# Attention scores on the two halves of TensorE's rows: near beside far products, and two sparse units together

## Chip, cores and metric

The kernel runs on one core of a Trainium2 chip. The metric is the device time of one execution in microseconds (us). TensorE multiplies, VectorE (DVE) and ScalarE (ACT) work on its results, SyncE (SP) issues the loads of weights; GpSimd (POOL) does nothing.

## What is computed

The program is three blocks on an activation of 512 positions by 1024 features in f32: a convolution layer, a layer of dilated attention, and a layer with a sparse attention and an mLSTM between two feed-forward parts. The change touches two spots.

The dilated attention has 8 heads of 64 features in each of three groups (window, dilation): (128, 1), (512, 4), (2048, 16). A softmax for each group, weighted over the groups by their log denominators, is the same as one softmax over all keys of the three groups:

```python
s = jnp.einsum('bdnqhc,bdnkhc->bdnhqk', qb, kk) * (hd ** -0.5)
s = jnp.where(valid[:, None], s, NEG_INF)      # 0 <= dist <= band, in the residue's own subsequence
...
wts = jax.nn.softmax(jnp.stack(lses, axis=0), axis=0)
o = jnp.sum(wts[..., None] * jnp.stack(outs, axis=0), axis=0)
```

The sparse attention has 8 query heads on 2 heads of keys; every query attends its 128 best keys by an index score:

```python
score = jnp.einsum('bqhs,bqh->bqs', jax.nn.relu(jnp.einsum('bqhd,bsd->bqhs', iq_blk, ik)), iw_blk)
top_s, top_i = lax.top_k(score, k_sel)
s = jnp.einsum('bqgrd,bqkgd->bqgrk', q_blk, kg) * att_scale
```

## The kernel before

Each engine has one instruction stream, written out by hand; counters (semaphores) order them, and an engine waits in place, with all that is queued behind. Weight tiles of 128 x 1024 come through a ring of four: SyncE loads a tile, ScalarE copies its high part (`prep`, L444), VectorE subtracts to get the low part (L953), and TensorE makes 24 matmuls of 512 columns of it (`tile`, L1570).

**Dilated attention (stage 4).** Heads are taken two at a time, in four chunks; the two heads of a chunk lie on partitions 0 to 63 and 64 to 127 of `at_raw`. A chunk has 10 slots `j`, each with one weight tile of the input projection for chunk `c`, while the attention of the chunk before, `a = c - 1`, goes on beside it; the fourth attention chunk (`c == 4`) has no tiles beside it. An attention chunk has 8 units: unit `u` is head `u // 4` and residue `r = u % 4`, the 128 queries `r, r + 4, ...`. A unit's scores (`unit_scores`, L1753) are one near product, 128 queries by all 512 keys of group 0 into one PSUM bank (L1770), and two far products of 128 by 128 for groups 1 and 2 into the next bank (L1772). Both contract over 64 features, so they use half of TensorE's 128 rows, the head's own half; operands with a step of four are read as they lie.

VectorE adds the mask, scales, and takes the maximum of all 768 scores in one `tensor_tensor_reduce` (L1245), and negates it (L1248, `m_done`). ScalarE exponentiates with the row sum (L688, `e_done`); VectorE takes the reciprocal and scales (L1268, L1269, `p_done`). TensorE transposes the six blocks (L1798, `t_done`), ScalarE copies them to `at_PT`, and TensorE multiplies with the values (L1789). In slot `j` TensorE does, after the tile, the values of unit `j - 2`, the transposes of unit `j - 1`, the scores of unit `j`, and then a transpose of values (L1842) or a sum of squares (`sum_squares`, L1621). The scores of a unit wait for `m_done` of the unit before, whose bank they take; in the fourth chunk there are two homes, and the wait is for the unit before that.

In the slots behind a tile of queries or keys VectorE also makes the head norm and the rotary turn: L975 on the sum of squares, L968 to L970 (Newton, after ScalarE's guess L473, L474), L1276 to L1279 (`n_done`); tiles of values and gates it evacuates at L1265 and L1260. ScalarE copies a raw tile, squares it, and issues four DMAs that swap rows into `at_pair` (L725); from the third tile on the issue waits for `n_done` of the tile two before. Tiles of queries and keys are 0, 1, 3, 4, 5, 6 of a chunk; of values 2, 7, 8; of gates 9.

**Sparse attention (stage 10).** 32 units, `SPARSE_UNITS`, by block `b` of 128 queries (keys 0 to 128 (b + 1)), head column `c` and half: successive units lie on alternating halves. Iteration `u` of TensorE has the transposes of `u` (L2040), `scores(u + 2)` (L1950, product at L1955, after `m_done` of unit `u`), a weight tile if `u` is in `FILL`, and the values of `u - 1` (L2056). VectorE has in iteration `u` `normalise(u + 1)` (L1370), `masked(u + 2)` (L1357), the tile's low part and rounds of the top selection. The first two units' scores stand together in stage 9. The index scores (L1945) alternate halves too.

Of the kernel before, what the change touches and what calls it, by code (L numbers as in the profile page):

```python
# [19 lines left out]
P = 128  # L20
S = 512
# [10 lines left out]
HEAD = 64  # L32
# [110 lines left out]
TIMES = {"chunk": 4 * len(QK_TILES), "unit": 4 * UNITS}  # L143


def build(nc, weights, x_in, ple_in, pos_in, params_in, consts_in, masks_in, out, spill):
    ctx = ExitStack()
    with ctx:
# [41 lines left out]
        with ExitStack() as s_first:  # L190
# [3 lines left out]
            with ExitStack() as s_conv:  # L194
# [8 lines left out]
            (at_raw, at_pair, at_mask, at_T, at_SG, at_Sm, at_PT, at_st, at_Yh, at_Yl, at_V) = scope(  # L203
                ("at_raw", [P, 12, S], F32), ("at_pair", [P, 2, S], F32), ("at_mask", [P, 4, 768], F32),
                ("at_T", [P, 2, S], F32), ("at_SG", [P, 2, S], F32),
                ("at_Sm", [P, 768], F32), ("at_PT", [P, 768], F32), ("at_st", [P, 4, 4], F32),
# [59 lines left out]
        s_done = sem("s_done")  # L266
        m_done = sem("m_done")
# [52 lines left out]
        def unit_home(a, u):  # L320

            if a == 3 and u % 2:
                return 0, at_raw[:, 0:2, :].rearrange("p a s -> p (a s)")[:, 0:768]
            return 2, at_Sm[:, :]
# [43 lines left out]
        def attention_over(k, chunk=(), unit=()):  # L368

            for kind, sems in (("chunk", chunk), ("unit", unit)):  # L370
                for s in sems:
                    k.n[s] = k.n.get(s, 0) + TIMES[kind]

# [51 lines left out]
        def _(act):  # L425
# [242 lines left out]
            act.dma_start(at_mask[:, :, :], masks_in).then_inc(mask_loaded, 16)  # L668
            k.up(dve_out)
            normed = k.n[n_done]  # L670
            for c in range(5):
                a = c - 1
                for j in range(SLOTS):
# [5 lines left out]
                    for step in ((1, 2) if c == 4 else (2, 1)):  # L679
# [5 lines left out]
                        else:  # L685
                            act.wait_ge(m_done, UNITS * a + j)
                            st, probs = at_st[:, (j - 1) % 4, :], unit_home(a, j - 1)[1]
# [251 lines left out]
        def _(dve):  # L939
# [293 lines left out]
            for c in range(5):  # L1233
                a = c - 1
                for j in range(SLOTS):
                    if c < 4 and j - 1 in SUM_SLOT:
                        head_var(1)
                    if a >= 0 and 0 <= j - 1 < UNITS:
                        u = j - 1
                        st = at_st[:, u % 4, :]  # L1240
                        if u == 0 and a == 0:
                            dve.wait_ge(mask_loaded, 16)
                        dve.wait_ge(s_done, UNITS * a + u + 1)
                        bank, probs = unit_home(a, u)
                        link(dve.tensor_tensor_reduce(  # L1245
                            out=probs, in0=flat(ps[:, bank:bank + 2, :])[:, 0:768], in1=at_mask[:, u % 4, :],
                            scale=HEAD ** -0.5, scalar=TAKEN, op0=ALU.add, op1=ALU.max, accum_out=st[:, 0:1]))
                        dve.tensor_scalar(st[:, 1:2], st[:, 0:1], -1.0, None, ALU.mult).then_inc(m_done, 1)  # L1248
# [17 lines left out]
                    if a >= 0 and 0 <= j - 1 < UNITS:  # L1266
                        dve.wait_ge(e_done, UNITS * a + u + 1)
                        link(dve.reciprocal(st[:, 3:4], st[:, 2:3]))  # L1268
                        dve.tensor_scalar(probs, probs, st[:, 3:4], None, ALU.mult).then_inc(p_done, 1)  # L1269
# [14 lines left out]
            attention_over(k, unit=(s_done, m_done, e_done, p_done, t_done, o_done))  # L1284
# [267 lines left out]
        def _(pe):  # L1552
# [200 lines left out]
            def unit_scores(a, j):  # L1753

                if a < 0 or j >= UNITS:
                    return
                rows, r = slice(HEAD * (j // 4), HEAD * (j // 4) + HEAD), j % 4
                if j == 0:
                    pe.wait_ge(n_done, normed + len(QK_TILES) * (a + 1))
                elif a < 3:  # L1760
                    pe.wait_ge(m_done, UNITS * a + j)
                elif j == 1:
                    pe.wait_ge(read_out, k.at(read_out))
                    pe.wait_ge(v_copied, GROUPS * 4)
                    pe.wait_ge(var_done, 4 * len(QK_TILES))
                else:
                    pe.wait_ge(m_done, UNITS * a + j - 1)
                bank = unit_home(a, j)[0]
                q = 6 * (a % 2)
                pe.matmul(ps[:, bank, :], at_raw[rows, q, r:S:4], at_raw[rows, q + 1, :], start=True, stop=True)  # L1770
                for g in (1, 2):
                    mm = pe.matmul(ps[:, bank + 1, (g - 1) * P:g * P], at_raw[rows, q + 2 * g, r:S:4],  # L1772
                                   at_raw[rows, q + 2 * g + 1, r:S:4], start=True, stop=True)
                mm.then_inc(s_done, 1)

            def unit_values(a, j):

                if 0 <= j - 2 < UNITS:
                    u = j - 2
                    rows, r = slice(HEAD * (u // 4), HEAD * (u // 4) + HEAD), u % 4  # L1780
# [13 lines left out]
                if 0 <= j - 1 < UNITS:  # L1794
                    pe.wait_ge(p_done, UNITS * a + j)
                    probs = unit_home(a, j - 1)[1]
# [15 lines left out]
            for c in range(5):  # L1812
                a = c - 1
                for j in range(SLOTS):
# [12 lines left out]
                    if c == 4:  # L1827
                        unit_scores(a, j)
                    if a >= 0:
                        unit_values(a, j)  # L1830
                    if 0 <= a < 3:
                        unit_scores(a, j)
# [18 lines left out]
            attention_over(k, unit=(s_done, m_done, p_done, t_done, pt_done, o_done), chunk=(r0_done, rs_done, n_done, var_done))  # L1851
# [98 lines left out]
            def scores(u):  # L1950
                c, half, b = SPARSE_UNITS[u]
                rows = slice(HEAD * half, HEAD * half + HEAD)
                if u >= 2:
                    pe.wait_ge(m_done, k.up(m_done))
                pe.matmul(ps[:, 4 + u % 2, 0:P * (b + 1)], ds_U[rows, c, b * P:(b + 1) * P],  # L1955
# [79 lines left out]
            for u in range(33):  # L2035
# [8 lines left out]
                if u < 30:  # L2044
                    scores(u + 2)
# [212 lines left out]
```

## Time and profile before

| | us |
|---|---|
| median of three runs | 2011.47 (2009.0 to 2016.49) |
| profiled execution | 2012.62 |
| its span | 2010.8 |
| TensorE matmuls busy | 1948.5 (97%) |
| weight loads | 1515.0 (75%) |
| VectorE | 1245.3 (62%) |
| ScalarE | 862.2 (43%) |
| mean granted clock of TensorE | 0.985 |

The profile gives for each instruction its start and length. PE is TensorE's matmul side, PEld its weight loads; an f32 product is two passes, each a load and a matmul record. Matmul records overlap with their successors by 0.07 us or more, so what a group costs is read from its start to the start of what follows. A granted clock of 1.00 is 2.4 GHz, of 0.50 1.2 GHz. The idle time before an instruction stands in brackets with what ended it.

### The profile page before, as it was taken

The numbers are of one execution on the slowest core, as the hardware profiler recorded it, in microseconds if no ns is written. First come the engines' busy times: TensorE is split into PE (matmuls) and PEld (weight loads), VectorE is DVE, ScalarE is ACT, GpSimd is POOL, SyncE is SP. The second block draws the span as 40 slices with busy tenths as digits, with TensorE's granted clock in tenths as the row PEclk, the third lists the DMA queues.
The fourth block names the chain that finished last, engine by engine and source line by source line (L and its number), as shares of the span: only waits on it lengthen the run. The fifth ranks groups of instructions, "written<-read, shape, count | busy, mean of one in ns | idle before, by whom it ended". The sixth has DMA issues, their size and how long they took to land.

```text
span 2010.8 us, 23124 instructions
## 1 busy us (share of the span) xinstructions
PE 1948.5 (97%) x8436; PEld 1515.0 (75%) x8436; DVE 1245.3 (62%) x1864; ACT 862.2 (43%) x1175; POOL 0.2 (0%) x4
## 2 busy tenths in 40 slices
PE   6999899899999999999999999999999999999999
PEld 4888687677777777888888876666766788888887
DVE  5999888757575738644443365588666555444322
ACT  5444555444444435544432234455343444434221
POOL 0000000000000000000000000000000000000000
PEclk9999999999999989999999999999999999999999
DMA  4333243221212112323333332112221223233333
GB/s 176 101 95 95 74 131 121 85 69 50 65 56 66 48 53 95 97 91 104 94 94 121 120 95 74 53 42 63 74 64 42 95 93 106 94 103 95 101 99 105
DMA packets 49281, 175.70 MB, mean 87 GB/s; under 512 B 6064, under 2 KB 6192, under 8 KB 48432
## 3 DMA queue, kind: packets, MB, share of 16 engines
q1 hardware_dynamic: 44640, 160.19, 25.5%
q10 hardware_dynamic: 4560, 14.41, 2.1%
q8 instruction: 53, 0.87, 0.2%
q14 instruction: 28, 0.23, 0.0%
HBM read 166.71 MB, written 6.29 MB: 86 GB/s over the span
## 4 chain that ended last, share of the span: by engine, by line
PE 72%; DVE 20%; ACT 5%; issue 2%; DMA 1%; ACTq 1%; DVEq 0%
PE ps L1570 58%; DVE cv_acc L1132 6%; DVE w_lo L953 3%; PE ps L1770 2%; PE ps L1621 2%; PE ps L1798 1%; PE ps L1772 1%; PE ps L1586 1%; PE ps L1789 1%; PE ps L1955 1%; ACT w_hi L435 1%; PE ps L2056 1%; DMA X<-x 1%; PE ps L1945 1%; DVE X L1005 1%
## 5 line engine op out<-in xcount | busy, mean ns | idle before, releaser
L953 DVE TENSOR_TENSOR w_lo<-w_raw,w_hi 128x1024 fp32r<-128x1024 f32 x299 | 365.6, 1224 | 365.1 <-ACT w_hi L435 359.2
L1570 PE MATMUL ps<-H_hi,w_hi 128*128 128x512 f32 x1272 | 509.4, 401 | 1.1 <-DVE H_lo L999 1.1
L1570 PE MATMUL ps<-H_hi,w_lo 128*128 128x512 f32 x1272 | 496.1, 390 | 0.0
L1570 PE MATMUL ps<-H_lo,w_hi 128*128 128x512 f32 x1272 | 496.0, 390 | 0.0
L435 ACT ACTIVATE w_hi<-w_raw 128x1024 fp32r<-128x1024 f32 x299 | 313.5, 1050 | 244.1 <-PE ps L1570 168.8
L1570 PEld LDWEIGHTS ps<-H_hi,w_hi 128*128 128x128 f32 x1272 | 239.5, 188 | 57.9 <-issue 7.4
L1570 PEld LDWEIGHTS ps<-H_lo,w_hi 128*128 128x128 f32 x1272 | 239.4, 188 | 55.3 <-issue 6.7
L1570 PEld LDWEIGHTS ps<-H_hi,w_lo 128*128 128x128 f32 x1272 | 239.2, 188 | 51.0
L1570 PE MATMUL ps<-mid_hi,w_lo 128*128 128x512 f32 x352 | 138.7, 394 | 0.0
L1570 PE MATMUL ps<-mid_hi,w_hi 128*128 128x512 f32 x352 | 138.7, 394 | 0.0
L1570 PE MATMUL ps<-mid_lo,w_hi 128*128 128x512 f32 x352 | 138.7, 394 | 0.0
L1570 PE MATMUL ps<-N_hi,w_hi 128*128 128x512 f32 x280 | 118.4, 423 | 0.7 <-ACT ds_P L815 0.7
L1132 DVE SCALAR_TENSOR_TENSOR cv_acc<-cv_a,par,cv_acc 128x509 f32<-128x509 f32 (+21 forms) x176 | 115.8, 725 | 1.6 <-ACT cv_acc L586 1.6
L1570 PE MATMUL ps<-N_lo,w_hi 128*128 128x512 f32 x280 | 111.6, 399 | 0.0
L1570 PE MATMUL ps<-N_hi,w_lo 128*128 128x512 f32 x280 | 111.5, 398 | 0.0
L435 ACT ACTIVATE mid_hi<-tmp 128x512 f32 x44 | 27.8, 632 | 193.2 <-DVE tmp L1090 193.2
L1570 PEld LDWEIGHTS ps<-mid_hi,w_hi 128*128 128x128 f32 x352 | 65.8, 187 | 16.5
L1570 PEld LDWEIGHTS ps<-mid_hi,w_lo 128*128 128x128 f32 x352 | 65.8, 187 | 16.2
L1570 PEld LDWEIGHTS ps<-mid_lo,w_hi 128*128 128x128 f32 x352 | 65.8, 187 | 16.2
L1086 DVE TENSOR_TENSOR tmp<-ps,rx 128x512 f32<-128x512 f32 x44 | 30.4, 691 | 66.1 <-PE ps L1570 66.1
L1570 PEld LDWEIGHTS ps<-N_hi,w_hi 128*128 128x128 f32 x280 | 53.4, 191 | 23.3 <-issue 9.5
L1570 PEld LDWEIGHTS ps<-N_lo,w_hi 128*128 128x128 f32 x280 | 53.4, 191 | 13.8 <-issue 2.4
(337 smaller groups left out, 2705.3 us busy)
## 6 DMA issues: line engine op xcount, KB each, us to landing
w_raw<-weights SPq DMA_DIRECT2D x299, 512.0 KB, 3.5
X<-x ACTq DMA_DIRECT2D x4, 512.0 KB, 11.3
pl_P<-spill ACTq DMA_DIRECT2D x1, 2048.0 KB, 7.9
spill<-X ACTq DMA_DIRECT2D x8, 256.0 KB, 2.0
X<-spill ACTq DMA_DIRECT2D x2, 1024.0 KB, 5.0
out<-X SPq DMA_DIRECT2D x8, 256.0 KB, 4.6
at_mask<-masks ACTq DMA_DIRECT2D x1, 1536.0 KB, 6.0
at_pair<-at_raw ACTq DMA_DIRECT2D x96, 16.0 KB
```

The costliest lines, as they stand in the source:

```text
L435: return act.activation(out_ap, in_ap, ACT.Copy)
L953: dve.tensor_tensor(w_lo[:, s, :], w_raw[:, s, :], w_hi[:, s, :].bitcast(F32), ALU.subtract)\
L1005: dve.scalar_tensor_tensor(X[:, m:m + n, :], src, scale, X[:, m:m + n, :], ALU.mult, ALU.add)\
L1086: dve.tensor_tensor(tmp[:, j, :], ps[:, bank_of(k.n["prep"] - AHEAD - 1), :], rx[:, :], ALU.mult).then_inc(read_out, 1)
L1132: instr = dve.scalar_tensor_tensor(acc, a[:, 0:S - t], w, acc, ALU.mult, ALU.add)
L1570: mm = pe.matmul(ps[:, bank, :], w, x, start=first and n == 0 and q == 0, stop=last and n == len(blocks) - 1 and q == 2)
L1586: mm = pe.matmul(ps[:, banks[which], :], w, x[:, b, :], start=b == 0 and q == 0, stop=b == KC - 1 and q == 2, skip_group_check=True)
L1621: pe.matmul(ps[:, bank, :], ones if lhsT is None else lhsT, sq[:, (k.n[sq_done] - 1) % 2, :], start=c == 0, stop=c == n - 1).then_inc(sq_u ...
L1770: pe.matmul(ps[:, bank, :], at_raw[rows, q, r:S:4], at_raw[rows, q + 1, :], start=True, stop=True)
L1772: mm = pe.matmul(ps[:, bank + 1, (g - 1) * P:g * P], at_raw[rows, q + 2 * g, r:S:4], at_raw[rows, q + 2 * g + 1, r:S:4], start=True, stop= ...
L1789: mm = pe.matmul(ps[rows, 6, r * P + q0:r * P + q1], at_V[:, 3 * (a % 2) + g, v * P + rows.start:v * P + rows.stop], at_PT[:, b * P + q0:b ...
L1798: mm = pe.transpose(ps[:, 4 + b // 4, (b % 4) * P:(b % 4 + 1) * P], probs[:, b * P:(b + 1) * P], ident)
```

## The change

In the dilated attention a unit `u` is now head `u % 2` and residue `u // 2` (`unit_rows`). TensorE's stream has nine steps -1 to 7 in a chunk: step `v` has the near product of unit `v + 1` and the far products of unit `v`, which lie on different halves of the rows and in different banks. Step -1 stands at the end of slot 9 of the chunk before. A near product waits for `near_done` of the bank's last reader, the far ones for `m_done`. VectorE reduces the near and the far part in two instructions, in successive slots, and joins the two maxima. The probabilities have two buffers in the first three chunks, three in the fourth. The mask is held as `at_near` (4 x 512) and one `at_far` (256) and comes in two DMAs. In the sparse attention `two_scores` makes the products of two units one behind the other, at even `u`, after `m_done` of both units before.

```diff
-TIMES = {"chunk": 4 * len(QK_TILES), "unit": 4 * UNITS}
+TIMES = {"chunk": 4 * len(QK_TILES), "unit": 4 * UNITS, "step": 4 * (UNITS + 1)}
...
-            (at_raw, at_pair, at_mask, at_T, at_SG, at_Sm, at_PT, at_st, at_Yh, at_Yl, at_V) = scope(
-                ("at_raw", [P, 12, S], F32), ("at_pair", [P, 2, S], F32), ("at_mask", [P, 4, 768], F32),
+            (at_raw, at_pair, at_near, at_far, at_T, at_SG, at_Sm, at_PT, at_st, at_Yh, at_Yl, at_V) = scope(
+                ("at_raw", [P, 12, S], F32), ("at_pair", [P, 2, S], F32), ("at_near", [P, 4, S], F32), ("at_far", [P, 2 * P], F32),
                 ("at_T", [P, 2, S], F32), ("at_SG", [P, 2, S], F32),
-                ("at_Sm", [P, 768], F32), ("at_PT", [P, 768], F32), ("at_st", [P, 4, 4], F32),
+                ("at_Sm", [P, 2, 768], F32), ("at_PT", [P, 768], F32), ("at_st", [P, 4, 4], F32),
...
         def unit_home(a, u):
 
-            if a == 3 and u % 2:
-                return 0, at_raw[:, 0:2, :].rearrange("p a s -> p (a s)")[:, 0:768]
-            return 2, at_Sm[:, :]
+            if a == 3 and u % 3 == 2:
+                return at_raw[:, 0:2, :].rearrange("p a s -> p (a s)")[:, 0:768]
+            return at_Sm[:, (u % 3 if a == 3 else u % 2), :]
+
+        def unit_rows(u):
+            return slice(HEAD * (u % 2), HEAD * (u % 2) + HEAD), u // 2
+
+        def near_bank(a, u):
+            return 0 if a == 3 and u >= 3 and u % 2 else 2
+
+        def far_bank(a, u):
+            return 1 if a == 3 and u % 2 else 3
...
-            act.dma_start(at_mask[:, :, :], masks_in).then_inc(mask_loaded, 16)
+            act.dma_start(at_near[:, :, :], masks_in[:, :, 0:S]).then_inc(mask_loaded, 16)
+            act.dma_start(at_far[:, :], masks_in[:, 0, S:S + 2 * P]).then_inc(mask_loaded, 16)
...
-                    if a >= 0 and 0 <= j - 1 < UNITS:
+                    if a >= 0 and 0 <= j <= UNITS:
                         u = j - 1
-                        st = at_st[:, u % 4, :]
-                        if u == 0 and a == 0:
-                            dve.wait_ge(mask_loaded, 16)
-                        dve.wait_ge(s_done, UNITS * a + u + 1)
-                        bank, probs = unit_home(a, u)
-                        link(dve.tensor_tensor_reduce(
-                            out=probs, in0=flat(ps[:, bank:bank + 2, :])[:, 0:768], in1=at_mask[:, u % 4, :],
-                            scale=HEAD ** -0.5, scalar=TAKEN, op0=ALU.add, op1=ALU.max, accum_out=st[:, 0:1]))
-                        dve.tensor_scalar(st[:, 1:2], st[:, 0:1], -1.0, None, ALU.mult).then_inc(m_done, 1)
+                        if u < 0 and a == 0:
+                            dve.wait_ge(mask_loaded, 32)
+                        dve.wait_ge(s_done, (UNITS + 1) * a + j + 1)
+                        if u >= 0:
+                            st, probs = at_st[:, u % 4, :], unit_home(a, u)
+                            link(dve.tensor_tensor_reduce(
+                                out=probs[:, S:S + 2 * P], in0=ps[:, far_bank(a, u), 0:2 * P], in1=at_far[:, :],
+                                scale=HEAD ** -0.5, scalar=TAKEN, op0=ALU.add, op1=ALU.max, accum_out=st[:, 3:4]))
+                            dve.wait_ge(near_done, UNITS * a + u + 1)
+                            link(dve.tensor_tensor(st[:, 0:1], st[:, 0:1], st[:, 3:4], ALU.max))
+                            dve.tensor_scalar(st[:, 1:2], st[:, 0:1], -1.0, None, ALU.mult).then_inc(m_done, 1)
+                        if j < UNITS:
+                            dve.tensor_tensor_reduce(
+                                out=unit_home(a, j)[:, 0:S], in0=ps[:, near_bank(a, j), :], in1=at_near[:, j // 2, :],
+                                scale=HEAD ** -0.5, scalar=TAKEN, op0=ALU.add, op1=ALU.max,
+                                accum_out=at_st[:, j % 4, 0:1]).then_inc(near_done, 1)
...
-            def unit_scores(a, j):
-
-                if a < 0 or j >= UNITS:
-                    return
-                rows, r = slice(HEAD * (j // 4), HEAD * (j // 4) + HEAD), j % 4
-                if j == 0:
-                    pe.wait_ge(n_done, normed + len(QK_TILES) * (a + 1))
-                elif a < 3:
-                    pe.wait_ge(m_done, UNITS * a + j)
-                elif j == 1:
-                    pe.wait_ge(read_out, k.at(read_out))
-                    pe.wait_ge(v_copied, GROUPS * 4)
-                    pe.wait_ge(var_done, 4 * len(QK_TILES))
-                else:
-                    pe.wait_ge(m_done, UNITS * a + j - 1)
-                bank = unit_home(a, j)[0]
+            def step_scores(a, v):
+
+                near, far = (v + 1 if v + 1 < UNITS else None), (v if v >= 0 else None)
                 q = 6 * (a % 2)
-                pe.matmul(ps[:, bank, :], at_raw[rows, q, r:S:4], at_raw[rows, q + 1, :], start=True, stop=True)
-                for g in (1, 2):
-                    mm = pe.matmul(ps[:, bank + 1, (g - 1) * P:g * P], at_raw[rows, q + 2 * g, r:S:4],
-                                   at_raw[rows, q + 2 * g + 1, r:S:4], start=True, stop=True)
+                if near is not None:
+                    rows, r = unit_rows(near)
+                    if near == 0:
+                        pe.wait_ge(n_done, normed + len(QK_TILES) * a + 2)
+                    if a == 3 and near == 3:
+                        pe.wait_ge(read_out, k.at(read_out))
+                    elif UNITS * a + near:
+                        pe.wait_ge(near_done, UNITS * a + near - (a == 3 and near > 3))
+                    mm = pe.matmul(ps[:, near_bank(a, near), :], at_raw[rows, q, r:S:4], at_raw[rows, q + 1, :],
+                                   start=True, stop=True)
+                if far is not None:
+                    rows, r = unit_rows(far)
+                    if far == 0:
+                        pe.wait_ge(n_done, normed + len(QK_TILES) * (a + 1))
+                    if a == 3 and far == 1:
+                        pe.wait_ge(v_copied, GROUPS * 4)
+                        pe.wait_ge(var_done, 4 * len(QK_TILES))
+                    elif UNITS * a + far:
+                        pe.wait_ge(m_done, UNITS * a + far - (a == 3 and far > 1))
+                    for g in (1, 2):
+                        mm = pe.matmul(ps[:, far_bank(a, far), (g - 1) * P:g * P], at_raw[rows, q + 2 * g, r:S:4],
+                                       at_raw[rows, q + 2 * g + 1, r:S:4], start=True, stop=True)
                 mm.then_inc(s_done, 1)
...
-                    rows, r = slice(HEAD * (u // 4), HEAD * (u // 4) + HEAD), u % 4
+                    rows, r = unit_rows(u)
...
-                    if c == 4:
-                        unit_scores(a, j)
+                    if c == 4 and j < UNITS:
+                        step_scores(a, j)
                     if a >= 0:
                         unit_values(a, j)
-                    if 0 <= a < 3:
-                        unit_scores(a, j)
+                    if 0 <= a < 3 and j < UNITS:
+                        step_scores(a, j)
...
+                    if c < 4 and j == SLOTS - 1:
+                        step_scores(c, -1)
...
-            def scores(u):
-                c, half, b = SPARSE_UNITS[u]
-                rows = slice(HEAD * half, HEAD * half + HEAD)
-                if u >= 2:
-                    pe.wait_ge(m_done, k.up(m_done))
-                pe.matmul(ps[:, 4 + u % 2, 0:P * (b + 1)], ds_U[rows, c, b * P:(b + 1) * P],
-                          ds_kvi[rows, 0, 0:P * (b + 1)], start=True, stop=True).then_inc(s_done, 1)
-                k.up(s_done)
+            def two_scores(first):
+
+                if first:
+                    pe.wait_ge(m_done, k.up(m_done, 2))
+                for u in (first, first + 1):
+                    c, half, b = SPARSE_UNITS[u]
+                    rows = slice(HEAD * half, HEAD * half + HEAD)
+                    pe.matmul(ps[:, 4 + u % 2, 0:P * (b + 1)], ds_U[rows, c, b * P:(b + 1) * P],
+                              ds_kvi[rows, 0, 0:P * (b + 1)], start=True, stop=True).then_inc(s_done, 1)
+                    k.up(s_done)
...
-                if u < 30:
-                    scores(u + 2)
+                if u < 30 and u % 2 == 0:
+                    two_scores(u + 2)
```

The counters' totals in `attention_over` and the callers of `unit_home` follow.

## Rows read from the trace of the kernel before

**Rows 1.** Stretches: length, then busy us (records) by engine, granted clock, DMA share, GB/s.

```profile
412.70:508.70 96.00, 94.53 (x458) 73.90 (x457) 63.15 (x104) 43.89 (x65) 0.00 (x0) 1.00 0.21 62
...
700.40:720.90 20.50, 19.88 (x78) 14.93 (x78) 7.91 (x21) 6.43 (x11) 0.00 (x0) 0.50 0.00 1
...
1484.90:1576.40 91.50, 86.77 (x415) 58.27 (x414) 53.27 (x143) 42.26 (x86) 0.00 (x0) 1.00 0.14 42
```

**Rows 2.** The chain of waits between 540 and 600 us: start, length, what.

```profile
551.78 5.47 PE ps L1570 x24
...
572.67 5.49 PE ps L1570 x24
...
578.98 0.63 DVE at_Sm L1269
```

**Rows 3.** Timeline of one unit's scores, TensorE and its weight loads: start, length.

```profile
528.12 1.24 PE L1770 MATMUL ps<-at_raw 64*128 64x512 f32 x2
...
529.21 1.08 PE L1772 MATMUL ps<-at_raw 64*128 64x128 f32 x4
...
530.22 1.13 PE L1621 MATMUL ps<-sq,con 128*128 128x512 f32 x2
...
528.78 1.21 PEld L1772 LDWEIGHTS ps<-at_raw 64*128 64x128 f32 x4
```

**Rows 4.** Timeline, TensorE: sparse and index scores, with transposes and values.

```profile
1251.89 0.49 PE L1945 MATMUL ps<-ds_kvi,X 64*128 64x256 f32 x2
...
1415.16 0.49 PE L1955 MATMUL ps<-ds_kvi,X 64*128 64x128 f32 x4
...
1427.79 0.48 PE L1955 MATMUL ps<-ds_kvi,X 64*128 64x128 f32 x2
...
1550.08 0.66 PE L2040 MATMUL ps<-con,ds_P 128*128 128x128 f32 x4
...
1550.66 1.12 PE L1955 MATMUL ps<-ds_kvi,X 64*128 64x512 f32 x2
...
1551.72 1.09 PE L2056 MATMUL ps<-ds_PT,ds_kvi 128*64 128x128 f32 x8
```

**Rows 5.** Groups by line and shape, VectorE: busy us, mean ns, idle before.

```profile
L1245 DVE CUSTOM_DVE_ANT_0 at_Sm<-ps,at_mask 128x768 f32<-128x768 f32 x28 | 26.8, 957 | 13.4 <-PE ps L1772 12.7
...
L1248 DVE TENSOR_SCALAR at_st<-at_st 128x1 f32<-128x1 f32 x32 | 4.9, 154 | 1.1
...
L1364 DVE CUSTOM_DVE_ANT_0 ds_P<-ps,ds_acc 128x512 f32<-128x512 f32 x8 | 5.5, 686 | 7.3 <-PE ps L1955 7.3
...
L1364 DVE CUSTOM_DVE_ANT_0 ds_P<-ps,ds_acc 128x256 f32<-128x256 f32 x8 | 3.4, 420 | 3.9 <-PE ps L1955 3.9
```

**Rows 6.** Timeline of slots 5 to 7, VectorE and ScalarE (ACTq issues DMAs).

```profile
555.98 0.69 DVE L968 TENSOR_TENSOR rs<-r 128x512 f32<-128x512 f32 x1 [0.37 <-ACT r L474]
...
560.93 2.62 ACTq L725 DMA_DIRECT2D at_pair<-at_raw  x4
...
572.50 2.62 ACTq L725 DMA_DIRECT2D at_pair<-at_raw  x4
...
577.71 0.19 ACT L688 ACTIVATION_READ_ACCUMULATOR at_Sm<-at_Sm,at_st 128x1 f32 x1
```

**Rows 7.** Timeline of the fourth chunk's units, TensorE.

```profile
701.02 1.54 PE L1798 MATMUL ps<-con,at_Sm 128*128 128x128 f32 x6 [2.00 <-DVE at_Sm L1269]
...
702.49 2.09 PE L1770 MATMUL ps<-at_raw 64*128 64x512 f32 x2
...
721.08 1.25 PE L1770 MATMUL ps<-at_raw 64*128 64x512 f32 x2
...
725.00 1.25 PE L1770 MATMUL ps<-at_raw 64*128 64x512 f32 x2
```

**Rows 8.** Timeline, VectorE: reductions of two successive sparse units.

```profile
1558.88 0.68 DVE L1364 CUSTOM_DVE_ANT_0 ds_P<-ps,ds_acc 128x512 f32<-128x512 f32 x1
...
1561.23 0.68 DVE L1364 CUSTOM_DVE_ANT_0 ds_P<-ps,ds_acc 128x512 f32<-128x512 f32 x1
```

More of the change, by code:

```diff
@@ L266, in build @@
         s_done = sem("s_done")
+        near_done = sem("near_done")
         m_done = sem("m_done")
@@ L366, in build, with attention_over @@
         V0 = GROUPS * 4
-        def attention_over(k, chunk=(), unit=()):
-            for kind, sems in (("chunk", chunk), ("unit", unit)):
+        def attention_over(k, chunk=(), unit=(), step=()):
+            for kind, sems in (("chunk", chunk), ("unit", unit), ("step", step)):
                 for s in sems:
@@ L686, in _ @@
                             act.wait_ge(m_done, UNITS * a + j)
-                            st, probs = at_st[:, (j - 1) % 4, :], unit_home(a, j - 1)[1]
+                            st, probs = at_st[:, (j - 1) % 4, :], unit_home(a, j - 1)
                             act.activation(probs, probs, ACT.Exp, bias=st[:, 1:2], accum_out=st[:, 2:3])\
@@ L1266, in _ @@
                     if a >= 0 and 0 <= j - 1 < UNITS:
+                        st, probs = at_st[:, u % 4, :], unit_home(a, u)
                         dve.wait_ge(e_done, UNITS * a + u + 1)
@@ L1283, in _ @@
             gate(3)
-            attention_over(k, unit=(s_done, m_done, e_done, p_done, t_done, o_done))
+            attention_over(k, unit=(near_done, m_done, e_done, p_done, t_done, o_done), step=(s_done,))
             stage_end(dve, "dve", k, 4)
@@ L1795, in unit_values @@
                     pe.wait_ge(p_done, UNITS * a + j)
-                    probs = unit_home(a, j - 1)[1]
+                    probs = unit_home(a, j - 1)
                     for b in range(6):
@@ L1850, in _ @@
                         sum_squares(0, 1, 1, head_ones)
-            attention_over(k, unit=(s_done, m_done, p_done, t_done, pt_done, o_done), chunk=(r0_done, rs_done, n_done, var_done))
+                    if c < 4 and j == SLOTS - 1:
+                        step_scores(c, -1)
+            attention_over(k, unit=(near_done, m_done, p_done, t_done, pt_done, o_done), step=(s_done,), chunk=(r0_done, rs_done, n_done, var_done))
             k.up(split_lo, 4)
@@ L1962, in _ @@
                     pe.wait_ge(n_done, k.at(n_done, 5))
-                    scores(0)
-                    scores(1)
+                    two_scores(0)
                 if s_ < len(MIX_TILES):
```

## Prediction

> **What bounds the kernel now.** I first cut the execution into stretches, to see which engine is full where the change acts. In a chunk of the dilated attention TensorE is busy for 94.5 of 96.0 us, VectorE for 63; in the second part of the sparse attention TensorE for 86.8 of 91.5 [rows 1]. TensorE's instruction stream is the bound, so time taken out of it counts until another engine's chain becomes the last to arrive. The chain of waits shows where that is near: it runs through TensorE, tile after tile (551.78, 572.67), and leaves it in this piece only for VectorE's evacuation and scaling of the probabilities, ahead of the transposes (0.63 at 578.98) [rows 2]. Then I read what a score group costs, and whether two row halves ever ran together.
>
> **The score products of the dilated attention.** A unit's near product begins at 528.12, its two far ones at 529.21, the next work at 530.22 [rows 3]: near 1.09, far 1.01, together 2.10 us, and 8 x 2.10 = 16.8 a chunk. Each product is two passes, a weight load before each; the far products' four loads span 1.21 us [rows 3], more than their columns need.
>
> Do two halves run at once? The kernel already contains such pairs. The first two sparse units (halves 0 and 1, nothing waited for between) take 0.49 us for four passes of 128 columns; one unit's two passes take 0.48 [rows 4]. In the index scores two passes of 256 columns began together and both took 0.49 [rows 4]. So pairs of equal size are free in their second member. The change's main pair is unequal, 512 columns beside two times 128, with strided weights: no row shows that. Its bounds are 1.09 (the near product alone) and 2.10 (nothing overlaps). I take 1.2: the far side's four loads become the longer stream, 1.21, and the equal pairs speak for the low end. A near or a far step alone I also put at 1.2, since neither now has the other to hide its first load and its tail.
>
> A chunk then has one near step alone (moved to slot 9 of the chunk before), seven pairs and one far step alone: 9 x 1.2 = 10.8, gross 6.0 saved.
>
> **What VectorE pays.** One reduction over 768 columns costs 0.957 us; two over 512 and 256 cost 0.686 + 0.420 (rows of the same operation in the sparse part), with a second accumulator read (0.08) and one more one-column operation (0.15, by the negation's row) [rows 5]: 1.34 + gaps instead of 0.96, +0.4 us a unit. It is hidden mostly: the negated maximum comes after the 256 columns, so ScalarE's exponential starts no later, and the near reduction runs while VectorE would wait for ScalarE (0.37 idle before L968) [rows 6]. If that cover were gone it would be 32 x 0.4 = 13 us. The new wait on near_done holds a product that needs its bank read; that reduction is done in the same VectorE slot, 5.5 us of weight tile earlier, in the first three chunks. The wait of VectorE on its own near_done is for work of the slot before: nothing.
>
> **What is late next.** In slots 5 and 6 ScalarE issues its four row-swap DMAs only when VectorE's rotary chain of an earlier tile has ended: issue at 560.93 and again at 572.50 [rows 6], 11.57 us apart, while the TensorE slot is 10.45 (two slots from 551.78 to 572.67) [rows 2]. This loop has no score product in it. It ends in the exponential, read out at 577.90; evacuation, reciprocal and scaling follow, and the probabilities could be ready near 579.0 instead of 579.6. TensorE alone would come 2 x 0.9 earlier. So of 1.8 us about 0.7 stays; 1.1 is given back as longer waits around slot 7. A chunk nets 6.0 - 1.1 = 4.9; three chunks **14.7 us**.
>
> The fourth chunk has no weight tiles beside it. Its start gains nothing: step -1, near reduction (0.7), then the first pair are in series, and the first transposes wait 2.00 us already (701.02) [rows 7]. Behind them stand six units' scores. At full clock a cycle of one unit is 3.92 us (721.08 to 725.00) [rows 7]; without 0.9 it would be 3.0, which is also VectorE's and ScalarE's chain (far reduction to maximum 0.9, exponential 1.1, scaling 0.9), so 0.9 is all there is. TensorE is at 1.2 GHz there for 20.5 us (granted 0.50) [rows 1], where a near product takes 2.09 instead of 1.25 [rows 7]; the shorter cycle puts more units into that stretch. 6 x 0.9 = 5.4, less 1.4 for that: **4.0 us**.
>
> **The sparse attention.** A single unit's score takes 1.06 us at 512 columns (1550.66 to 1551.72) and 0.42 at 128 [rows 4], between them by width 0.63 and 0.84. The first pair is a pair already. Of the other 15 pairs one member each goes: 3 x 0.42 + 4 x 0.63 + 4 x 0.84 + 4 x 1.06 = 11.4 gross. In the first eight units a weight tile stands in each, and their four pairs (1.9) are kept whole. For units 10 to 15 VectorE's rounds of the top selection end last: I count nothing. Beyond, VectorE's loop takes 2.35 us a unit (1558.88 to 1561.23) [rows 8], TensorE's 2.65 (score 1.06; values 1.09 and transposes 0.66, each less 0.07 of overlap with its successor) [rows 4]; a pair would bring it to 2.12, so only 0.30 of each 0.53 counts, 57% of 7.6 = 4.3. The new wait at even units, for the second unit's maximum, ends about 0.1 to 0.3 us behind the transposes where VectorE is late (reduction 0.69, negation 0.15) and costs nothing elsewhere; some 0.2 in all. 1.9 + 4.3 - 0.2: **6.0 us**, between 2 and 11.4.
>
> **Edits at nothing.** The mask in two DMAs (1.5 MB becomes 1.15, needed a chunk later); the third probability buffer; the new order of the units over halves and residues, which changes no size.
>
> **Sum.** 14.7 + 4.0 + 6.0 = 24.7 us from the profiled execution's 2012.6, which is 1.1 above the median of the runs: 1987.9, or 1987 against that median. A change under 0.5% (10 us) could not be told from none.
>
> **Rivals.** (1) *Passes keep their order of issue*: then a far pass can't begin before near's second, and the pair costs 1.09 / 2 + 1.01 = 1.55. A pair saves 0.55, a chunk 7 x 0.55 - 0.3 = 3.6, the four 14 less 3 for the start of the last and slots 5 to 7; the sparse pairs half, 3. Together 14: 1998. Against it: two index passes started within 0.01 us, while one unit's two passes are 0.21 apart (0.48 for two of 0.27), so those two were different heads, out of order [rows 4]. Chance 0.08. The Trainium skill states this rule in TensorE: Matmul & The Clock Gate, "The mechanism": starts and ends of matmuls follow program order and only weight loads are pulled ahead. By it the sum would be this rival's; the trace disagrees with it.
>
> (2) *The unequal, strided pair doesn't overlap*; the sparse ones do. Then the dilated part pays its rearrangement: the last chunk's serial start and the lost hiding, about +3, against -6: 2009. For it: no such pair in the trace. Chance 0.06.
>
> (3) *Slower, through the clock.* In the last chunk TensorE idled 2.00 us and its clock was at 1.2 GHz for the next 20.5 [rows 1, 7]. The same may follow the longer wait at slot 7 of three chunks, where today's short wait grows to some 1.5, split by the values. It decides once the idle time there comes to about 2 us. At 1.2 GHz a stretch of tiles does half its work: 10 us lost each, 31 for three, against 24.7: 2018. Against it: the chunks before are at full clock [rows 1] with such waits in them. Chance 0.04. If each lasts only a third as long, 10 us go: 1997, chance 0.06.
>
> **Numbers.** Forecast 0.76, its own range 1980 to 1995. Range of all: 1979 (near and far at the lower bound, more of the sparse 11.4) to 2001, which takes in rival 1 and the short clock falls and leaves out 2 and the long ones. Faster by over 0.5%: 0.76 + 0.07 + 0.05 = 0.88; within: rival 2 and edges 0.08; slower: 0.04.
>
> **What would show it.** Right: L1770's successor and the far matmuls starting together, pair to next work 1.1 to 1.3; chunk pitch 91 instead of 95.9; waits before the transposes or values at slot 7 grown to 1 to 2 us in all; the last chunk's unit cycle 3.0 to 3.2 at full clock; sparse units in pairs of one unit's duration. Wrong: far passes starting after near's second (rival 1) or after its end (2); granted clock under 0.95 in a chunk (3); or VectorE's reductions ending later than ScalarE's exponential, which would make the +0.4 a unit visible.

## The result, and the profile after

The changed kernel takes 1987.82 us (median of 4 runs, 1986.31 to 1989.35) against 2011.49 (2009.0 to 2016.49) for the kernel before: ratio 0.9873, 95% interval 0.9848 to 0.9898, 23.7 us less. The forecast was 1987.0, in a range of 1979 to 2001. The total came out right; two of its terms did not, and they nearly cancel. The profiled executions were 1.1 us above the median before and 1.5 below it after, so the traces differ by 26.3 us and not by 23.7.

The head of the page of the kernel after, to be held against the kernel before (span 2010.8, TensorE 1948.5 us, VectorE 1245.3):

```profile
span 1984.5 us, 23259 instructions
...
PE 1916.2 (97%) x8436; PEld 1495.0 (75%) x8436; DVE 1252.0 (63%) x1960; ACT 861.3 (43%) x1175; POOL 0.2 (0%) x4
```

TensorE has as many matmuls as before and is busy for 32 us less, for the most part because two of them now share a stretch of time; VectorE has 96 instructions and 7 us more. The changed pair itself, timeline of TensorE in the second attention chunk (start, length, with the line, shape and count), read in windows so narrow that passes are not merged. Line 1784 is the near product (1770 before), 1796 the far ones (1772), 1822 the transposes, 1640 the sum of squares, which comes next:

```profile
525.47 0.82 PE L1784 MATMUL ps<-at_raw 64*128 64x512 f32 x1
525.47 0.59 PE L1796 MATMUL ps<-at_raw 64*128 64x128 f32 x1
525.89 0.41 PE L1796 MATMUL ps<-at_raw 64*128 64x128 f32 x1
526.12 0.59 PE L1784 MATMUL ps<-at_raw 64*128 64x512 f32 x1
526.12 0.41 PE L1796 MATMUL ps<-at_raw 64*128 64x128 f32 x1
526.36 0.41 PE L1796 MATMUL ps<-at_raw 64*128 64x128 f32 x1
526.70 1.13 PE L1640 MATMUL ps<-sq,con 128*128 128x512 f32 x2
```

From 525.47 to 526.70 the pair takes 1.23 us; before, a unit's products took 2.10 [rows 3]. The near product's first pass and a far pass begin together at 525.47; a second far pass begins at 525.89, ahead of the near product's second at 526.12; the other two far ones begin at 526.12 and 526.36. The program issues both near passes before any far one, so the starts of passes on different row halves do not follow the program's order.

Stretches of the kernel after, with the columns of [rows 1]. The first goes from the tile of slot 0 in the second attention chunk to the same tile a chunk later; the others are the pieces at half clock between 405 and 740 us:

```profile
502.04:593.19 91.15, 89.04 (x458) 69.62 (x457) 64.97 (x128) 43.43 (x66) 0.00 (x0) 1.00 0.21 63
...
482.90:486.30 3.40, 3.40 (x7) 1.99 (x7) 3.26 (x6) 0.00 (x0) 0.00 (x0) 0.50 0.01 2
667.20:670.60 3.40, 3.40 (x9) 2.33 (x8) 3.26 (x6) 0.00 (x0) 0.00 (x0) 0.50 0.02 5
687.70:697.90 10.20, 8.05 (x34) 5.27 (x32) 6.33 (x24) 4.19 (x7) 0.00 (x0) 0.50 0.00 0
```

Between the same two tiles, with the same 458 matmuls, the kernel before takes 95.96 us (502.99 to 598.95): the chunk gains 4.8 us. But there are two short pieces at 1.2 GHz, at 482.9 and 667.2, in chunks that were wholly at 2.4 GHz before, and the long one in the fourth chunk is 10.2 us instead of 20.5.

What TensorE waits for between 360 and 760 us (waited for: us in total, times, longest), first in the kernel before, then after:

```profile
PE ps L1798 <- DVE at_Sm L1269: 6.4, 10, 2.0
PE ps L1842 <- DVE var L975: 4.3, 2, 4.1
PE ps L1621 <- DVE var L975: 2.1, 1, 2.1
PE ps L1789 <- ACT at_PT L435: 1.2, 1, 1.2
PE ps L1808 <- DVE at_Yl L1012: 0.3, 1, 0.3
```

```profile
PE ps L1822 <- DVE at_Sm L1288: 5.4, 9, 0.8
PE ps L1866 <- DVE var L986: 4.6, 2, 4.1
PE ps L1784 <- DVE at_st L1263: 2.9, 2, 2.2
PE ps L1640 <- DVE var L986: 2.1, 1, 2.1
PE ps L1605 <- DVE G_lo L1010: 2.1, 1, 2.1
PE ps L1813 <- ACT at_PT L445: 1.9, 4, 0.9
```

New are the wait of the near product on VectorE's near reduction (the serial start of the fourth chunk) and, in each of the first three chunks, a wait of the values on ScalarE. (The wait on `G_lo` is not new: the kernel before has it at 764.48, outside this window.) Slot 7 in the first attention chunk, timeline of TensorE:

```profile
478.72 1.09 PE L1813 MATMUL ps<-at_PT,at_V 128*64 128x128 f32 x12 [0.37 <-ACT at_PT L445]
480.62 0.88 PE L1822 MATMUL ps<-con,at_Sm 128*128 128x128 f32 x6 [0.80 <-DVE at_Sm L1288]
481.42 1.30 PE L1796 MATMUL ps<-at_raw 64*128 64x128 f32 x4
482.64 1.90 PE L1640 MATMUL ps<-sq,con 128*128 128x512 f32 x2
```

The waits are 0.37 + 0.80 = 1.17 us, and the work behind the far products, from 482.64, is at half speed (two passes in 1.90 us; 1.12 in the second chunk). ScalarE's issue loop, rows of its timeline after:

```profile
555.45 2.62 ACTq L736 DMA_DIRECT2D at_pair<-at_raw  x4
...
567.01 2.62 ACTq L736 DMA_DIRECT2D at_pair<-at_raw  x4
```

11.56 us apart, as in [rows 6] (11.57), while two TensorE slots there now take 9.59 each: the loop has not moved.

The fourth chunk at full clock, timeline of TensorE, first pass of three successive near products; the cycle is 3.06 us, against 3.92 in [rows 7]:

```profile
698.75 0.81 PE L1784 MATMUL ps<-at_raw 64*128 64x512 f32 x1
...
701.81 0.82 PE L1784 MATMUL ps<-at_raw 64*128 64x512 f32 x1
...
704.86 0.82 PE L1784 MATMUL ps<-at_raw 64*128 64x512 f32 x1
```

And a pair of sparse units with 512 columns each, four passes where [rows 4] had two in 1.12; the next work begins 1.06 us after them:

```profile
1528.34 1.13 PE L1983 MATMUL ps<-ds_kvi,X 64*128 64x512 f32 x4
1529.40 1.09 PE L2083 MATMUL ps<-ds_PT,ds_kvi 128*64 128x128 f32 x8
1531.57 0.66 PE L2067 MATMUL ps<-con,ds_P 128*128 128x128 f32 x4 [1.08 <-DVE ds_P L1393]
```

**Where the time went.** I read the start of the same weight tile in both traces, profiled execution against profiled execution (26.3 us less span). From the tile at 398.98 before (399.69 after) to the one at 687.72 (677.47) the three chunks gain 0.71 + 10.25 = 11.0 us. The fourth chunk, from there to 743.11 (724.04), gains 8.8. The sparse units gain 6.6. The three sum to 26.4. Behind waits of 1.14 and 1.54 us on VectorE's scaling, the sparse stretch of this trace has a short piece at half clock of its own:

```profile
1483.00:1486.40 3.40, 3.40 (x9) 2.63 (x9) 1.65 (x5) 1.92 (x4) 0.00 (x0) 0.50 0.00 0
```

The profiles of experiments 3, 4 and 5 have the same sparse code and the same two waits, and no such piece there; between the same tiles they gain 7.6, 8.05 and 7.96 us.

### The profile page after: what moved, and what is told of

The parts are those of the page before. It is cut to its first block, busy times and chain, and to the rows that moved or that the text cites. A ratio compares the mean times of both kernels' runs of the same rounds, so it can differ in the third digit from the quotient of the medians.

```text
span 1984.5 us, 23259 instructions
## 1 busy us (share of the span) xinstructions
PE 1916.2 (97%) x8436; PEld 1495.0 (75%) x8436; DVE 1252.0 (63%) x1960; ACT 861.3 (43%) x1175; POOL 0.2 (0%) x4
## 4 chain that ended last, share of the span: by engine, by line
PE 75%; DVE 16%; ACT 5%; issue 2%; ACTq 2%; DMA 1%; DVEq 0%
PE ps L1589 63%; DVE w_lo L964 2%; PE ps L1605 2%; ACTq L736 1%; PE ps L1640 1%; ACT w_hi L445 1%; PE ps L1784 1%; PE ps L1822 1%; PE ps L1813 1%; PE ps L1796 1%; DVE cv_acc L1143 1%; DMA X<-x 1%; DVE rs L980 1%; DVE rs L981 1%; PE ps L1971 1%
```

## The experiments

Each is timed against the kernel before on the same chip. "Dilated gain" and "sparse gain" are read at the same tiles as above.

**1. Dilated part alone.** The sparse attention has its single scores back.

```
-                if u < 30 and u % 2 == 0:
-                    two_scores(u + 2)
+                if u < 30:
+                    scores(u + 2)
```

> The dilated part as changed, the sparse scores one unit at a time as before. If the two parts are independent, the time is 6.6 us over the changed kernel's (the sparse stretch's loss in the two traces): 1994, and the 64 sparse passes run two by two again, 1.12 for 512 columns. If the gain of the two parts were shared (one clock state, one chain), it would be under 3 or over 10.

Measured: 1994.07 us, ratio 0.9903 (0.9876 to 0.993). Dilated gain 19.9, sparse gain 0.

**2. Sparse part alone.** The kernel before, with `two_scores` for its `scores` and the wait for two maxima.

> The sparse part as changed, the dilated one as before. Independent parts: 2011.5 - 6.6 = 2005. With the whole gross of 11.4 (if VectorE took nothing back) 2000. The stretch from the first score to the last transposes should be that of the changed kernel to 0.5 us.

Measured: 2005.31 us, ratio 0.9961 (0.9946 to 0.9977). Sparse gain 6.6. By the ratios the two parts save 1.0% and 0.4%, the change 1.3%: they do not touch each other.

**3. The new schedule without the overlap.** All steps, waits and split reductions of the change stay, but near and far units lie mostly on the same row half (one of the seven pairs of a chunk has both halves).

```
-            return slice(HEAD * (u % 2), HEAD * (u % 2) + HEAD), u // 2
+            return slice(HEAD * (u // 4), HEAD * (u // 4) + HEAD), u % 4
```

(and the mask of near scores is indexed by `j % 4`).

> The changed kernel with the units in the old order of halves (head u // 4, residue u % 4), so that near and far of a step lie on the same half, but for one step in eight; everything else of the change stays: the steps, the waits, the split reductions, the moved near step. If the overlap of halves makes the gain, a step costs 2.1 again, the chunk 95.5 to 97 instead of 91.2, and the time is 2005 to 2008 (the sparse 6.6 stays), some 3 us over the rival's bound of the old dilated part. If the rearrangement makes it, the time stays near 1988. If passes keep their order of issue, a step of different halves would cost 1.55 in the changed kernel, and this one would be only 9 us slower than it.

Measured: 2003.63 us, ratio 0.995 (0.9932 to 0.9968), 16 us slower than the change. The same instructions in the same order now run one after the other:

```profile
529.15 1.24 PE L1784 MATMUL ps<-at_raw 64*128 64x512 f32 x2
530.23 1.08 PE L1796 MATMUL ps<-at_raw 64*128 64x128 f32 x4
531.24 0.70 PE L1640 MATMUL ps<-sq,con 128*128 128x512 f32 x1
```

From 529.15 to 531.24 is 2.09 us, the price of before. So the gain comes from the two halves. The dilated gain is 5.0 us. In each of the first three chunks the rearrangement loses 1.33 us in slot 9, where a near product now stands alone, and gets 0.87 back in slot 7, where the far ones do; the one pair on both halves adds 0.87. So without any pair a chunk would lose 0.46 us; with the one it gains 0.41, 1.2 over three. The other 3.8 us come in the fourth chunk, whose piece at half clock was 13.7 us instead of 20.5 (experiment 6 shows what such a difference is worth). The rest of this run's gain is the sparse part's 7.6.

**4. A third row-swap buffer.** If ScalarE's issue loop gives back what slots 5 to 7 save, a third buffer should loosen it.

```
-                            if n >= 2:
-                                act.wait_ge(n_done, normed + n - 1)
+                            if n >= 3:
+                                act.wait_ge(n_done, normed + n - 2)
```

(the buffers become `n % 3`, with their semaphores).

> The changed kernel with a third buffer for the row swap, so that ScalarE's four DMAs wait for the rotary chain of three tiles before, not two. If that loop is what gives back 1.1 us a chunk, the waits of TensorE at slot 7 (0.33 before the values, 0.80 before the transposes) fall to the 0.49 of the tile's evacuation, a chunk becomes 0.7 to 0.9 shorter, 2.4 us over three, and the two idle times of TensorE in the first projection chunk (2.1 and 4.1 us, slots 7 and 8), if they hang on the same loop, go too: 1979 to 1983. If VectorE's added 0.4 us a unit is what comes late, nothing changes: 1988.

Measured: 1973.31 us, ratio 0.98 (0.9783 to 0.9818), 14.5 us below the change and 6 below the expectation. The two profiled executions differ by 11.7 us: 14.0 are gained between 379 us and the start of the fourth chunk, and 2.3 are lost elsewhere, where the code is the same and the clock fell at other places. TensorE's waits between 360 and 760 us:

```profile
PE ps L1827 <- DVE at_Sm L1293: 4.4, 9, 0.5
PE ps L1789 <- DVE at_st L1268: 3.1, 2, 2.3
PE ps L1610 <- DVE G_lo L1014: 2.1, 1, 2.1
PE ps L1871 <- DVE var L990: 1.1, 2, 0.8
PE ps L1818 <- ACT at_PT L449: 0.9, 1, 0.9
```

The wait on ScalarE's probabilities is left only in the fourth chunk, none of those behind VectorE's scaling is longer than 0.5, and one stretch of the page shows what that did to the clock (columns as in [rows 1]):

```profile
400.00:675.00 275.00, 269.78 (x1381) 210.83 (x1379) 196.05 (x388) 134.41 (x198) 0.00 (x0) 1.00 0.21 64
```

No piece at half clock is left in the three chunks. As the expectation put it with an "if", the waits of 2.1 and 4.1 us on the variance, in slots 7 and 8 of the projection chunk ahead of them in both kernels, are the same loop: 0.3 us of them is left. What was not expected is the clock: with the half clock behind these waits gone too, they brought 8.5 us, and the three chunks gave another 5.4: two short falls at 1.7 and three times 0.33 + 0.31 of waits.

**5. More work for VectorE.** One more operation over 256 columns behind each near reduction.

```
+                            dve.tensor_tensor(at_spare[:, 0:2 * P], at_far[:, :], at_far[:, :], ALU.add)
```

> The changed kernel with one more VectorE operation a unit (256 columns into a spare place, about 0.4 us), right behind the near reduction: the change's own added cost once more, 32 x 0.4 = 13 us of VectorE. If VectorE's added work is hidden but at slot 7, a chunk grows by 0.3 to 0.5 in its waits there, 1 to 2 us in all: 1989 to 1990. If VectorE is the bound, it grows by up to 13: 2000. If it is hidden everywhere: 1988.

Measured: 1988.6 us, ratio 0.9887 (0.987 to 0.9903), within the spread of the change's own runs. TensorE's wait on ScalarE's probabilities goes from 1.9 to 2.9 us over four places, the serial start of the fourth chunk from 2.9 to 3.5, the rest is as before. So of 13 us more work for VectorE 1.6 us show as waits and the rest is hidden. The total does not show them, also because this profile has a short fall of the clock in the first attention chunk only, one fewer than the change's, and none in the sparse part.

**6. The third buffer in the kernel before.** Is the loop a bound that the change uncovered, or an old one?

> The kernel before the change with the third buffer for the row swap. The changed kernel gained 14.5 us by it: 9 in the first projection chunk (idle time and a low clock behind it) and 5.5 in the other chunks and their clock. If the loop through ScalarE's DMAs became late only by the change's shorter slots, the other chunks gain nothing here and only the first does: 2011.5 - 9 = 2002 to 2003. If the loop held the old kernel as well, the gain is the same 14.5: 1997.

Measured: 2000.2 us, ratio 0.9937 (0.9921 to 0.9954). It gains 8.5 us between 379 and 407 us, in slots 7 and 8 of the projection chunk ahead of the attention; then nothing to 688 us; then 4.5 in the fourth chunk. So beside the attention the loop was just in time before, and only the shorter slots of the change make it late. The stretches at those slots, kernel before and then this one:

```profile
387.00:397.00 10.00, 6.59 (x26) 4.81 (x26) 6.64 (x10) 3.16 (x4) 0.00 (x0) 0.98 0.21 59
396.60:403.40 6.80, 5.17 (x15) 4.23 (x16) 6.56 (x11) 3.97 (x5) 0.00 (x0) 0.50 0.24 77
```

```profile
387.00:397.00 10.00, 9.69 (x45) 7.75 (x44) 9.66 (x15) 4.68 (x6) 0.00 (x0) 1.00 0.34 101
396.60:403.40 6.80, 6.80 (x33) 5.67 (x32) 4.65 (x7) 2.25 (x4) 0.00 (x0) 1.00 0.26 75
```

45 matmuls instead of 26 in the first ten microseconds, and a full clock behind them. The 4.5 us in the fourth chunk have no edit to explain them: its code is that of before. Its piece at half clock was 10.2 us instead of 20.5.

```profile
690.80:701.00 10.20, 8.21 (x33) 6.01 (x32) 5.06 (x15) 3.78 (x7) 0.00 (x0) 0.50 0.00 0
```

**7 and 8. The late selection rounds left out,** in the changed kernel and in the one before. Both leave out VectorE's top-selection rounds that stand at units 8, 10, 12 and 14, so that their selection is incomplete; it costs that much less.

```
-                **{u: ((3, 2),) for u in (8, 10, 12, 14)}, 17: ((3, 1),), 20: ((3, 1),)}
+                17: ((3, 1),), 20: ((3, 1),)}
```

> The changed kernel without the eight top selection rounds of units 8, 10, 12 and 14 (for the last block of queries). If they are what kept the pairs of units 10 to 15 from gaining, the stretch from unit 8's tile to the end of the sparse scores gets shorter by more than in the kernel before (next run): sparse gain 8.0 to 8.5 instead of 6.6; this kernel 3 to 4 us under the changed one.

> The kernel before without the same eight rounds. TensorE waited for VectorE there 0.47 and 1.08 us: it gets 1.5 us shorter, 2010. If the rounds have nothing to do with the pairs' loss, it gains as much as the changed kernel does by it.

Measured: 1982.87 us, ratio 0.9853 (0.9833 to 0.9873), and 2011.21, 0.9991 (0.998 to 1.0002). Between the same sparse tiles the first gains 11.9 us on the unaltered kernel before, more than the 8.0 to 8.5 expected, the second 2.0: without the rounds the pairing brings 9.9 us instead of 6.6. Not all of the difference is the rounds': the profile of number 7 has no half clock in this stretch, that of the change has the piece at 1483. Against the 8.0 of experiments 4 and 5, which have none either, the rounds hold back 1.9 us. Waits of TensorE on the scaled probabilities between 1390 and 1580 us, kernel after and then with the rounds left out:

```profile
PE ps L2067 <- DVE ds_P L1393: 6.0, 7, 1.5
```

```profile
PE ps L2067 <- DVE ds_P L1393: 2.9, 4, 1.1
```

These two runs were worth as much for the clock, since their dilated part is untouched code. Number 8 repeats the kernel before in it. It has a short fall in the second attention chunk, where no wait between 510 and 534 us is longer than 0.49, and its half clock in the fourth chunk was again the short one, at the same wait of 2.00 us:

```profile
530.80:534.20 3.40, 3.40 (x7) 2.00 (x7) 2.99 (x5) 0.00 (x0) 0.00 (x0) 0.50 0.00 0
701.50:711.70 10.20, 8.46 (x31) 6.29 (x32) 4.50 (x12) 4.22 (x8) 0.00 (x0) 0.50 0.00 0
```

It gained 4.3 us in the fourth chunk. Number 7 repeats the changed kernel and had the short fall of the first attention chunk but not that of the third; there it is 1.7 us ahead of the change's own profile at the same tile.

**9. Scaling ahead of the evacuation,** on top of experiment 4. In slots 2, 7 and 8 VectorE evacuates a value tile before it scales the probabilities, and TensorE waits 0.49 us each time.

```
+                    if a >= 0 and 0 <= j - 1 < UNITS:
+                        (wait, reciprocal and scaling, from 10 lines below)
                     if c < 4:
                         (evacuation of the tile)
-                    if a >= 0 and 0 <= j - 1 < UNITS:
-                        (wait, reciprocal and scaling)
```

> The kernel with the third row-swap buffer waits nine times on VectorE's scaling of the probabilities, 0.49 us each, 4.4 us in all, at slots 2, 7 and 8 of the first three chunks, where VectorE first evacuates the value tile (0.69 us) and then scales. Here VectorE scales first, in those slots and all others. If these waits are on the path: 1973.3 - 4.4 = 1969 us. Rival: the evacuation, now 0.9 us later, holds the bank or the V transposes instead, and the time stays at 1973 or above, with new waits behind the variance or the value evacuation. A second rival, from the clock rows: nothing changes in the granted clock, since waits of 0.5 us were never followed by a fall; if the clock gains beyond that, the time goes below 1968.

Measured: 1969.76 us, ratio 0.979 (0.9773 to 0.9806), 3.6 below experiment 4. The two were timed on different chips and their ratios differ by 0.1% only, inside the intervals; but between the same tiles of the two profiles, from 407 to 743 us, the gain is 4.35 us, which is nine waits of 0.49. The line of the scaling is gone from TensorE's waits between 360 and 760 us, and the rest is nearly unchanged:

```profile
PE ps L1790 <- DVE at_st L1268: 3.1, 2, 2.3
PE ps L1611 <- DVE G_lo L1014: 2.5, 2, 2.1
PE ps L1872 <- DVE var L990: 1.2, 2, 0.8
PE ps L1819 <- ACT at_PT L449: 0.9, 1, 0.9
PE ps L1653 <- DVE var L1003: 0.5, 1, 0.5
```

This is the fastest version, 41.6 us under the kernel before and 18 under the changed one.

## Why the prediction was right, and where it was not

**The pair, 1.2 us: right.** It measured 1.23, nearest to the far loads' 1.21 that the prediction took from [rows 3]. A far step alone measured 1.23 too (574.23 to 575.46, slot 7 of the second chunk). A near step alone took 1.17 (407.99 to the next work), but its slot grew by more: the first one from 8.06 to 9.48, 1.4 us and in part at half clock, the two later ones by 1.35 and 1.33.

**A chunk, 4.9 net: right.** The second attention chunk, undisturbed, went from 95.96 to 91.15. The give-back was forecast at 1.1, "as longer waits around slot 7"; they are 0.33 for the values and 0.80, instead of 0.5, for the transposes. Experiments 4 and 6 show the cause that the prediction named, the row swaps' issue loop: loosened, it pays in the changed kernel's chunks and not in the old one's.

**Three chunks, 14.7: too much.** They gave 11.0. 3 x 4.8 = 14.4 stands; two short falls of the clock took 1.7 us each, 3.4. The step that failed is the sum's assumption that these chunks stay at full clock. It was rival 3's mechanism in its short form: the waits at slot 7 grew, and 1.2 GHz followed them in two chunks of three. The rival's price was a third of 10 us for each; it measured half of that. Its condition, about 2 us of idle time, was too high: 1.17 us preceded the fall at 482.9. The same 1.1 us of waits were followed by none in the second chunk, and by none in the third of experiments 5 and 7, so the wait does not alone decide it. Over all profiles: of the twelve chunks with these waits (the change and experiments 1, 5 and 7, three chunks each) six had such a fall; of the 21 of the other seven profiles, with no wait above 0.5 us, one had it, the one of experiment 8. So such falls go with these waits, most of all in the first chunk (four of four), and one came without; the expectation of experiment 9, that waits of 0.5 us are never followed by a fall, is wrong by that one.

**The fourth chunk, 4.0: too little.** It gave 8.8. The step that failed is the clock's term: the prediction held the 20.5 us at half clock fixed and charged 1.4 us because more units would run in them. The cycle at full clock is 3.06 us against 3.0 forecast. The piece at 1.2 GHz was 10.2 us. Runs 6 and 8, with the fourth chunk as it was before, show that this length is no property of the code: 20.5 in the profiles of the kernel before and of experiment 2, 10.2 in those of 6 and 8, worth 4.5 and 4.3 us. Nor did it follow from the length of the wait, 2.0 us in all four; the clock fell 1.4 us after the wait's start in the first two, and 0.6 ahead of it and 0.2 after it in the other two. No run varied that. Take 4.5 off and 4.3 is left for the shorter cycles, against 4.0. The profiles of the change and of experiments 1, 4, 5, 7 and 9 all had some 10 us; whether it follows from the change, or was chance as for the old one, stays open.

**The sparse part, 6.0: near, with some luck.** It gave 6.6: 2.6 in the first eight units (forecast 1.9), 0.1 while the late rounds run (forecast 0), 3.9 beyond (4.3). The last has the short fall at 1483 in it; without one the same code gave 8.0, 5.3 of it beyond the rounds. So at full clock the term was 2 us too low, and the sum had no term for the clock here either. The 1.9 us that the prediction gave up for VectorE's rounds is what experiments 7 and 8 show (9.9 without them against 8.0). Why the first units gained 0.7 and the last ones 1.0 more than forecast was not tried.

**VectorE's 0.4 us a unit, mostly hidden: right**, by experiment 5, which adds as much again and finds 1.6 us of 13 as waits.

**Rival 1, order of issue: refuted.** Two far passes start ahead of the near product's second, and the pair takes 1.23 us, not the 1.55 of this rival. The Trainium skill (TensorE: Matmul & The Clock Gate, "The mechanism") has it that matmuls start and end in the program's order and that only weight loads are pulled ahead; for passes on different row halves the trace disagrees (525.89 ahead of 526.12). **Rival 2, no overlap of an unequal strided pair: refuted** by the same rows. Its price for the bare rearrangement, 3 us of loss, was too high for what experiment 3 shows: 0.46 a chunk, 1.4 over the first three. In the fourth that run gained 3.8, with a half clock 6.8 us shorter, so a loss there can't be told.

So the misses were -3.7 (three chunks), +4.8 (the fourth) and +0.6 (the sparse part), the first two of the clock. They leave 1.7 us, 26.4 against the 24.7 forecast, and the profiled execution of the change happened to be the fastest of its four, 1.5 us under the median. The mechanism was right; that the median was hit within 1 us was partly luck.

## What to carry to other kernels

Matmuls that use half of the rows are worth pairing even when they are of unequal width: here the pair cost 1.23 us, as much as the longer of its two members alone (near 1.17, far 1.23), and the test is to put both on the same half. When a full engine is made shorter, look for the loop of the other engines whose period is close to its slot; here one more buffer for that loop brought 14.5 us, more than half of what the change itself did. Of that, 5.4 us came from the slots that the change had shortened; 8.5 us had been there for the taking before it. And sum such a chunk's profile with the clock's pieces kept apart, since they change by several microseconds between executions of the same code.

## What the runs showed of the hardware that was not expected

- Passes on different row halves start out of the program's order: a second far pass at 525.89, with the near product's second still to come at 526.12.
- A stretch at 1.2 GHz came in lengths of 3.4, 6.8, 10.2, 13.7 and 20.5 us in this part of the kernel. The same code at the same wait of 2.0 us had 20.5 in two profiles and 10.2 in two others. A fall of 3.4 us cost 1.7 us beside the attention; one followed waits of 0.37 and 0.80 us, and one a wait of 0.49.
- Taking away waits of 2.1 and 4.1 us brought 8.5 us, more than their sum of 6.2, since a piece at half clock of 6.8 us went with them.
